# Down projection of a mixture of experts with the tokens stationary and w_down streaming, on one Trainium2 core

## The reference

```python
logits = (xf @ w_router + b_router).astype(jnp.float32)      # xf = rmsnorm(x), (1024, 1024)
top_logits, top_idx = lax.top_k(logits, TOP_K)               # 4 of 32
top_w = jax.nn.softmax(top_logits, axis=-1)
...
def expert_block(args):
    xb, e = args
    gu = xb @ w_gate_up[e] + b_gate_up[e]
    gate = jnp.minimum(gu[:, 0::2], SWIGLU_LIMIT)
    up = jnp.clip(gu[:, 1::2], -SWIGLU_LIMIT, SWIGLU_LIMIT)
    hidden = (up + 1.0) * gate * jax.nn.sigmoid(SWIGLU_ALPHA * gate)
    return hidden @ w_down[e] + b_down[e]
...
y = jax.ops.segment_sum(y_slots * slot_w[:, None], slot_tok, num_segments=t)   # x + y is the result
```

## Time and profile before

| | |
|---|---|
| Median of three runs | 2355.8 us (2354.04 to 2357.43) |
| The profiled execution | 2354.11 us, span 2352.3 us, granted clock 0.986 |
| PE busy | 2256.7 us, 96% of the span |
| DVE, ACT, POOL busy | 940.0, 459.4, 222.8 us |
| DMA | 504.04 MB, mean 214 GB/s |
| Loop over blocks | from 672.7 us to the end |

### The profile page before, as it was taken

One profiled execution on the slowest core, in us unless ns is written; L12 is line 12 of the kernel. 1 busy time (PEld: TensorE's weight loads), 2 busy tenths in 40 slices (PEclk: granted clock), 3 DMA queues, 4 the chain that ended last, 5 costly groups with the idle time before them and its releaser, 6 DMA issues.

```text
span 2352.3 us, 43438 instructions
## 1 busy us (share of the span) xinstructions
PE 2256.7 (96%) x17777; PEld 2150.1 (91%) x17778; DVE 940.0 (40%) x2192; ACT 459.4 (20%) x848; POOL 222.8 (9%) x172
## 2 busy tenths in 40 slices
PE   6999998999969999999999999999999999999997
PEld 5878887778869999999999999999999999999997
DVE  6434434885363333233333333333333333333332
ACT  4243233664111111111111111111111111111110
POOL 1101100100001100001011000100010010001001
PEclk9999999999979999999999999999999999999999
DMA  4222221205377887788888878887888887888882
GB/s 164 99 72 72 90 81 61 75 3 196 129 230 250 276 282 239 238 274 263 290 278 278 281 239 274 266 279 228 289 273 290 277 255 236 285 290 271 290 274 36
DMA packets 250614, 504.04 MB, mean 214 GB/s; under 512 B 7994, under 2 KB 36718, under 8 KB 250238
## 3 DMA queue, kind: packets, MB, share of 16 engines
q1 hardware_dynamic: 234268, 451.96, 55.1%
q0 software_dynamic: 14912, 45.71, 9.7%
q10 hardware_dynamic: 1344, 5.01, 0.7%
HBM read 469.46 MB, written 31.10 MB: 213 GB/s over the span
## 4 chain that ended last, share of the span: by engine, by line
PE 91%; DVE 4%; issue 3%; DMA 2%; ACT 1%; POOL 0%; DVEq 0%; ACTq 0%; SPq 0%; POOLq 0%
PE bank L1044 43%; PE bank L1055 19%; PE bank L802 12%; PE bank L1032 2%; DVE hx L1407 2%; PE bank L1003 2%; PE bank L913 2%; PE bank L900 2%; PE bank L947 1%; PE bank L948 1%; PE bank L949 1%; PE bank L995 1%; DMA mix<-xn_scratch,hx 1%; PE bank L884 1%; PE bank L810 1%
## 5 line engine op out<-in xcount | busy, mean ns | idle before, releaser
L1044 PE MATMUL bank<-hx,ring 128*128 128x140 f32 (+1 forms) x8192 | 1034.3, 288 | 21.9 <-issue 12.5
L1044 PEld LDWEIGHTS bank<-hx,ring 128*128 128x128 f32 x8192 | 1018.5, 197 | 28.6 <-issue 27.6
L1055 PE MATMUL bank<-hx,ring 128*128 128x140 f32 (+1 forms) x4096 | 514.8, 287 | 0.0
L1055 PEld LDWEIGHTS bank<-hx,ring 128*128 128x128 f32 x4096 | 507.0, 190 | 0.0
L758 ACT ACTIVATE hx<-hx 128x168 f32<-128x168 f32 x256 | 87.9, 343 | 1439.1 <-DVE hx L1478 1439.1
L1478 DVE TENSOR_SCALAR hx<-bank,hx 128x168 f32<-128x168 f32 x256 | 100.4, 392 | 630.6 <-PE bank L1044 630.0
L1503 DVE TENSOR_SCALAR hx<-bank,hx 128x168 f32<-128x168 f32 x256 | 100.4, 392 | 354.2 <-PE bank L1055 354.2
L571 POOL DMA_INDIRECT out_x<-mix,hx x66 | 99.8, 1511 | 815.9 <-ACT mix L751 775.7
L550 POOL DMA_INDIRECT mix<-xn_scratch,hx x66 | 65.0, 984 | 719.0 <-DVE hx L1402 708.9
L802 PE MATMUL bank<-hx_r,mix_r 128*128 128x512 f32 x480 | 115.7, 400 | 7.6 <-DVE hx_r L1138 7.6
L802 PEld LDWEIGHTS bank<-hx_r,mix_r 128*128 128x128 f32 x480 | 91.8, 193 | 28.2 <-issue 9.1
(11 more groups left out here) (201 smaller groups left out, 1715.0 us busy)
## 6 DMA issues: line engine op xcount, KB each, us to landing
ring<-in_w_gate_up SPq DMA_DIRECT2D x128, 2048.0 KB, 11.1
ring<-in_w_down SPq DMA_DIRECT2D x64, 2048.0 KB, 8.9
mix<-in_w_in SPq DMA_DIRECT2D x14, 1024.0 KB, 5.0
work<-in_w_in SPq DMA_DIRECT2D x14, 1024.0 KB, 5.0
ring<-in_x SPq DMA_DIRECT2D x8, 512.0 KB, 8.3
hx<-in_w_out SPq DMA_DIRECT2D x1, 4096.0 KB, 14.3
work<-in_x ACTq DMA_DIRECT2D x8, 512.0 KB, 4.9
out_x<-work SPq DMA_DIRECT2D x8, 512.0 KB, 4.4
```

What stands on the lines that cost most here:

```text
L1044: mm = e.matmul(bank[f % 2][:, part * CAP:part * CAP + w], gu_ring[:, k, f * 256 + part:(f + 1) * 256:2], xT[:, k, 0:w], start=k == 0, sto ...
L1055: return e.matmul(bank[2 + j % 2][:, 0:w], dn_ring[:, k, j * P:(j + 1) * P], hid[:, k, 0:w], start=k == 0, stop=k == KD - 1)
```

## The change

Down now has the hidden tokens stationary (128 of them) and w_down moving, 512 columns at a time, in two halves t of the output and eight steps k. Both operands are split into a high fp32r part and a low rest, and three fp32r products are summed (`down_main`). The high part of w_down is copied by ScalarE (`upper`), the low one made by VectorE (`lower`), both in the gate and up part of the same block; `hid` is split likewise (`hid_hi`, `hidden_low`). The result lies with tokens on the partitions, so `turn_rows` and `yT` go, and `weigh_rows` scales it straight out of PSUM. The bias b_down enters by one more product (`down_bias`, three bf16 parts picked by `sel`). Tokens past 128 are handled in groups of 32 (RO = 2 groups): `down_over` multiplies 32 stationary tokens with four quarters of w_down's columns, each quarter in its own 32 columns of the array and 32 partitions of bank 7, in float32, behind a branch on the number of tokens. So these tokens are gathered and scattered as quarter rows of 256 elements. `hot` grows to 3 x 128 slots; there are three indirect DMAs for two, and the gather stands ahead of the scatter. The list is made after f=3 and the one-hot behind f=1. `w_down` is loaded when the block before has done all of down. The widths 140 and 168 stay for gate and up, in two copies of the body.

The diff, cut to its core:

```diff
-        hid = region(hx, 0, KD, CAP)
+        hid = region(hx, 0, KD, SLOTS)
+        hid_lo = region(hx_r, 0, KD, SLOTS)[:, :, 0:P]
+        hid_hi = region(hx_r, 1536, KD, P)
+        hot = region(work[:, 8192:9728].bitcast(BF16), 0, NT, NH * P)
+        dn_hi, dn_lo = region(work_r, 0, 2, KD, CH), region(mix_r, 0, 2, KD, CH)
...
                 for c in range(2):
-                    e.wait_ge(m_dn, n * 8 + (4 * c - 4))
+                    e.wait_ge(m_dn, n * 2 + 2)
                     e.dma_start(dn_ring[:, :, c * 512:(c + 1) * 512], dn_r[x_e, c]).then_inc(dn_in[c], 16)
...
             def block_dmas(n):
-                add_rows(n)
                 e.wait_ge(l_ok, n + 2)
-                e.wait_ge(g_tr, n * 3 + 3)
+                e.wait_ge(sc_done, n * 48 + 48)
                 e.sem_inc(pool_go, 1)
                 gather()
+                add_rows(n)
...
+            def upper(n, q):
+                nh, k = q // 4, q % 4 * 2
+                if k == 0:
+                    e.wait_ge(dn_in[nh], n * 16 + 16)
+                e.activation(dn_hi[:, nh, k:k + 2], dn_ring[:, k:k + 2, nh * CH:(nh + 1) * CH], ACT.Copy).then_inc(c_hi, 1)
...
             def weigh_rows(n):
-                e.wait_ge(sc_done, n * 32 + 16)
-                for h in range(2):
-                    for q in range(2):
-                        m = 2 * h + q
-                        e.wait_ge(m_ytr, n * 4 + (m + 1))
-                        e.activation(yo[:, h, q * 512:(q + 1) * 512], bank[4 + m][0:HC, :], ACT.Copy,
-                                     scale=w_sc[:, h:h + 1]).then_inc(m_yo, 1)
+                e.wait_ge(l_keep, n + 1)
+                e.wait_ge(g_tr, n * 4 + 8)
+                for t in range(2):
+                    e.wait_ge(m_dn, n * 2 + (t + 3))
+                    e.activation(y_m[:, t * CH:(t + 1) * CH], bank[2 + t][:, :], ACT.Copy, scale=w_sc[:, 0:1]).then_inc(m_yo, 1)
+                for r in range(RO):
+                    e.activation(y_o[:, r], bank[7][:, r * 2 * P:(r + 1) * 2 * P], ACT.Copy,
+                                 scale=w_sc[:, 1 + r:2 + r]).then_inc(m_yo, 1)
...
                     e.activation(sg[:, f % 2], g1[:, f % 2], ACT.Sigmoid, scale=GALPHA).then_inc(m_sig, 1)
-                    if f == 0:
-                        weigh_rows(n)
+                    if f == 3:
+                        upper(n, 0)
+                    if 3 <= f < 7:
+                        upper(n, f - 2)
+                    e.wait_ge(m_hid, n * 8 + (f + 3))
+                    e.activation(hid_hi[:, f], hid[:, f, 0:P], ACT.Copy).then_inc(h_hi, 1)
+                for q in range(5, 8):
+                    upper(n, q)
+                weigh_rows(n)
...
+            def down_bias(t):
+                e.matmul(bank[2 + t][:, :], sel, bias_d[:, t * CH:(t + 1) * CH], start=True, stop=False,
+                         skip_group_check=True)
+            def over_bias():
+                for r in range(RO):
+                    for j in range(GR):
+                        e.matmul(bank[7][quarter_rows(j), r * 2 * P:(r + 1) * 2 * P], sel[:, 0:OV],
+                                 bias_d[:, j * 2 * P:(j + 1) * 2 * P], start=r == 0, stop=False, skip_group_check=True)
+            def down_main(n, t, k):
+                if t == 0:
+                    e.wait_ge(h_lo, n * 8 + (k + 1))
+                if k % 2 == 0:
+                    e.wait_ge(c_lo, n * 8 + (4 * t + k // 2 + 1))
+                for h, w in ((hid_hi, dn_hi), (hid_lo, dn_hi), (hid_hi, dn_lo)):
+                    mm = e.matmul(bank[2 + t][:, :], h[:, k], w[:, t, k], start=False, stop=k == KD - 1 and w is dn_lo,
+                                  skip_group_check=True)
+                if k == KD - 1:
+                    mm.then_inc(m_dn, 1)
+            def down_over(r):
+                for k in range(KD):
+                    for j in range(GR):
+                        e.matmul(bank[7][quarter_rows(j), r * 2 * P:(r + 1) * 2 * P],
+                                 hid[:, k, P + r * OV:P + (r + 1) * OV], dn_ring[:, k, j * 2 * P:(j + 1) * 2 * P],
+                                 start=False, stop=k == KD - 1, skip_group_check=True)
...
+                e.wait_ge(s_sel, n + 1)
+                down_bias(0)
...
+                down_bias(1)
+                for k in range(4):
+                    down_main(n, 1, k)
+                e.wait_ge(g_in, n * 48 + 96)
+                turn_tokens()
+                for k in range(4, KD - 1):
+                    down_main(n, 1, k)
+                e.wait_ge(l_ok, n + 2)
+                over_bias()
+                with e.If(tokens > P):
+                    down_over(0)
+                if w > P + OV:
+                    with e.If(tokens > P + OV):
+                        down_over(1)
+                down_main(n, 1, KD - 1)
...
+            def lower(n, q):
+                nh, k = q // 4, q % 4 * 2
+                e.wait_ge(c_hi, n * 8 + (q + 1))
+                e.tensor_tensor(dn_lo[:, nh, k:k + 2], dn_ring[:, k:k + 2, nh * CH:(nh + 1) * CH],
+                                dn_hi[:, nh, k:k + 2].bitcast(F32), ALU.subtract).then_inc(c_lo, 1)
...
+                    if f == 3:
+                        lower(n, 0)
+                    if 3 <= f < 7:
+                        lower(n, f - 2)
```

More of the change, by code:

```diff
@@ L50 @@
 NE = 32
+OV = 32
+GR = P // OV
+RO = 2
 CAP = 168
-HC = CAP // 2
+SLOTS = P + RO * OV
+NH = 1 + RO
 TOPK = 4
@@ new lines, in layer @@
+        tw_s = region(hx[:, 7444:7444 + NT * 5 // 2].bitcast(BF16), 0, NT, 5)
+        pos_s = region(hx, 7464, NT)
+        pos_t = region(small, 840, NT)
+        it_base = region(hx, 7472, NI)
+        it_low = region(hx, 7472 + NI, NI)
+        it_f = region(hx, 7472 + 2 * NI, 2, NI)
+        it_i = region(hx, 7472 + 4 * NI, 2, NI).bitcast(I32)
+        btab = region(small, 224, NE, 16)
+        be = region(small, 736, 16)
+        l_raw = region(small, 752, NH)
+        idx = small[:, 756:756 + NH].bitcast(U32)
@@ L556, in _ @@
             e.wait_ge(e_st[1], 128)
-            e.dma_start(b_rows[:, 2048:3072], b_down[0]).then_inc(sc_done, 16)
+            for g in range(3):
+                e.dma_start(b_raw[g * NE:(g + 1) * NE], b_down[0]).then_inc(sc_done, 16)
             e.wait_ge(l_ok, 1)
@@ L992, in token_list @@
             def token_list():
-                for h in range(2):
+                for h in range(NH):
                     for i in range(NT):
-                        mm = e.matmul(bank[7][0:HC, 5 * h:5 * h + 5], hot[:, i, h * HC:(h + 1) * HC], tw_s[:, i, :],
+                        mm = e.matmul(bank[7][:, 5 * h:5 * h + 5], hot[:, i, h * P:(h + 1) * P], tw_s[:, i, :],
                                       start=i == 0, stop=i == NT - 1)
@@ L1104, in _ @@
                     block_pe(n)
-            turn_rows(more + NE)
         @block.vector
@@ L1438, in _ @@
             e.wait_ge(bias_ok, 3)
-            for m in range(3):
-                e.wait_ge(g_tr, m + 1)
+            for g in range(1, 3):
+                e.wait_ge(b_cast, g)
+                rows = slice(0, 3 * NE) if g == 1 else slice(2 * NE, 3 * NE)
+                e.tensor_tensor(b_raw[rows], b_raw[rows], bias_d[rows], ALU.subtract).then_inc(b_sub, 1)
+            for m in range(4):
+                e.wait_ge(g_tr, m + 1 if m < 2 else 4)
                 tokens_out(m)
-            for s_ in (m_up, m_gs, m_hid):
+            for s_ in (m_up, m_gs, m_hid, m_dn):
                 e.sem_inc(s_, 2)
+            e.sem_inc(m_yo, 4)
             grid = [P, NX, NE]
@@ L1499, in block_dve @@
                         list_out(n + 1)
-                e.wait_ge(m_ytr, n * 4 + 4)
-                for j in range(KD):
-                    e.wait_ge(m_dn, n * 8 + (j + 1))
-                    e.tensor_scalar(yT[:, j, :], bank[2 + j % 2][:, 0:CAP], be[:, 16 + j:17 + j], None, ALU.add)\
-                        .then_inc(m_y, 1)
-                    if j == 6:
-                        for m in range(3):
-                            e.wait_ge(g_tr, n * 3 + (m + 4))
-                            tokens_out(m)
+                hidden_low(n, KD - 1)
+                for q in range(5, 8):
+                    lower(n, q)
+                for m in range(4):
+                    e.wait_ge(g_tr, n * 4 + (m + 5 if m < 2 else 8))
+                    tokens_out(m)
             with e.Fori(0, NE) as n:
```

272 lines of the change are left out of this document (136 added, 136 removed).

## The result

The kernel after takes 2245.5 us (median of four runs, 2241.65 to 2247.83) against 2354.9 of the kernel before in the same session (2353.76 to 2357.43). The ratio is 0.9533, with an interval of 0.9521 to 0.9545: 4.7% faster. The forecast was 2260 with a range of 2240 to 2325, so the time lies in the range, 15 us under the forecast. The profiled execution took 2247.8, span 2246.0, against 2354.1 and 2352.3 before: 106.3 us of span less.

The account below looks back on a forecast made before the run. PE's own list was taken as the bound. Gains of 14 x 4.8, 13 x 0.9 and 18 for the wide blocks sum to 97 us; 2354.1 less 97 is 2257, taken as 2260, range 2240 to 2325.

Parts of the forecast that it names:

- second group of the 165 block: A second `down_over` call in the one block with more than 160 tokens, taken at 3.9 us.
- idle issue behind wide blocks: PE's idle issue at a wide block's end: 1.0 us left of the 1.96 now, in each of five blocks.
- What bounds it: PE's own list is the chain of waits, TensorE busy 96% of the span; a block is the sum of PE's pieces.
- the step on which it hung: In `down_over`, four column quarters overlap as two halves do: 3.9 us a call, 3.5 if all four overlap, 14.0 serially.
- The fp32r products: In `down_main`, 48 products of 512 columns a block at 0.2267 us each, 10.88 in all.
- the list: PE's part of making the list, each block: 24 small products for 16 which took 0.61, taken at 0.92 us.
- `over_bias`: Eight bias products of 256 columns in four column groups, every block: 0.9 us serially, 0.25 four at a time, taken 0.5.
- the branches: Branches in PE's loop body, each block: 0.1 us taken, 0 to 1.96 possible.
- rival 3: Waits in every block from late code, weights or DVE; 1.96 us in 27 more blocks, +53, 2313 us; chance 0.15.
- The cover: Added DVE (18 to 30 us a block), ACT (6 to 17) and transfer work costed at nothing; up to 64 us if gone.
- rival 4: DMA becomes the bound: by packets 51.0 us a narrow block, 103 more than the sum, 2363 us; chance 0.03.
- The ends: Kernel start 4 us later, finish 4 less (14.3 for 18.7 after the last product), so they cancel.

## Why the prediction was right, point by point

The loop's part of the sum, forecast against the trace of after (first product of block 0 to the last product):

| term | forecast | measured |
|---|---|---|
| 14 blocks up to 128 tokens | 45.3 each | 44.45 |
| 13 blocks of 129 to 140 | 49.2 each | 47.92 |
| 5 wide blocks, products alone | 55.2 each | 53.9 |
| second group of the 165 block | 3.9 | 3.46 |
| idle issue behind wide blocks | 5.0 | 16.5 |
| lower clock behind them | 0 | 11.7 |
| block 0, and the blocks at either end, beyond their kind | 0 | 9.2 |
| sum | 1558.7 | 1555.6 |

The 16.5 are what the block lengths leave; the four pieces of issue add up to 15.9, and each is 0.16 short, since a next product otherwise starts that much before the end of the last.

So 1555.6 for 1558.7 is errors that nearly cancel, and that is luck: 35 us too much on the blocks' own work, 23 too little behind the wide ones and 9 at the ends. The 9.2 are hardly a loss of the change: block 0 lasted 56.48 before and lasts 55.07 after. The kernel before had the like, some 8 us, which stood in its span. The forecast itself was a difference to that span, 97 us less; the pair of profiled executions shows 106.3 less, 105.3 in the loop and 1.0 at the ends. So the gain was 9.3 larger than forecast. The rest of the 15 us is 3 of rounding up to 2260 and 2.3 by which the profiled execution lies above the median.

**What bounds it** held: PE is the whole chain before and after. Every record removed came back at its price (12 transposes 1.31; 16 fp32r products 3.58). PE's idle time is in no block put down to ACT, DVE or DMA, except 1.5 in block 0, where DVE has only just made its tables.

**`down_over`, the step on which it hung**, held and to the lower bound: 3.46, where 3.9 was taken and 3.5 given as the end for all four. The step from halves to quarters was right. The page TensorE: Matmul & The Clock Gate of the Trainium skill gives, under "Measured speedup vs the span model", 2.38 times for three column tiles, from which the estimate was 4.4; here four quarters of float32 are at full rate. What the prediction didn't say is that the order of the loops is part of it: k outside and the quarters inside.

**The fp32r products** held: 24 in 5.46 are 0.2275 each for 0.2267, and all 48 in a block up to 128 tokens are 11.19 with the passing to quarters and back in them (5.46 + 2.75 + 2.09 + 0.89), for 10.88 + 0.2. Too dear were the list (0.59 for 0.92: 24 records cost no more than 16 did, so the price was not by the record), `over_bias` (0.33 for 0.5), the branches (0.1, none seen) and gate and up, 15.25 + 15.37 = 30.62 for 30.90. In the earlier trace rows gate and up came in three pieces, at 0.1275, 0.1193 and 0.1209 a record; now there are two, at 0.1191 and 0.1201, so a piece has a lead-in of its own that the turning back had added. All this is 0.85 a block, and with `down_over` 1.3.

**Behind the wide blocks lies the term that was most wrong in size.** One us of the 1.96 was left, behind each of five. Measured are 3.12 behind the 165 block, 4.13 to 4.31 behind three others and none behind the fifth, and in the block that follows a gap 2.8 to 3.0 more, since PE comes back at the lower clock: block lengths of 50.90 for 47.92 and 47.38 for 44.45. The mechanism stood in the prediction, under rival 3, but as a danger to the narrow blocks; there it didn't come. Two statements beside it were wrong. PE's loop does not keep its length (1784 for 1728), though this isn't what lengthened the gap, since the same 36 packets are fetched. And the gap is no fixed price of a jump: 5.3 to 6.2 us run from the first packet to the next product, and the new block leaves PE 1.3 us of work beside them where the old one left 4.0 to 4.2. The experiments with a shorter loop take the whole of it away. Which blocks of code are thrown out, and where between 1516 and 1680 the fetching begins, was not tried; nor is it shown why the wide block behind the 165 one has no gap.

**The cover** was rightly sized and wrongly placed. DVE 28.6 us a block for 30, ACT 15.8 for 17, `lower` 1223 ns and `upper` 1042 for 1.22 and 1.05. The prediction saw 3 us in hand, at f=2; at least 7.7 us more, spread over the block, fit under gate and up, and the thin place is the way from its end into `down_main`. The DMA share of 0.93 in a block of 44.44 us is 41.3, for 43.2 forecast from the earlier trace rows by bytes and 51.0 by packets (rival 4). The indirect queue alone has 13.3% of blocks that last 48 us on the mean, 6.4 us, where by packets it would be 15.6. So quarter rows don't cost as much as whole ones.

**The ends** did not cancel as told. At the start 0.9 later, not 4: the last gather's landing took 3.7 us, not 6.9. At the end the chain of waits has

```profile
2228.25 0.91 PE bank L1099 x3
...
2231.44 0.86 POOL out_x L603
...
2235.26 1.56 POOL out_x L606
```

From the last product (2229.16) to the last issue 6.1 us pass, against 6.2 forecast. But everything ends 10.7 later, not the 8.1 taken over from the earlier trace rows: 16.8 for 14.3, and 18.7 before. A scatter's median from issue to landing is 9.5 in the loop, 7.3 before. Start and end together gained 1.0.

## What to carry to other kernels

Where fewer than 128 stationary columns are left over, split the moving side into column groups and issue neighbours in different groups: the same products cost 3.46 or 11.31 us by the order of two loops. Count the instructions of a loop with branches over all copies of its body before adding a copy or a width, and keep what doesn't depend on the branch outside it; here that was worth 22 us, and one copy too many cost 267. Where a jump must fetch code, dear work just ahead of it hides the fetch and cheap work doesn't. A sum over TensorE's records was good to 3% a block here; the surprises stood where PE has nothing to do, so look at those first.

## What the runs showed of the hardware that was not expected

- Code fetches for TensorE's loop come in steps: none at 1400 and 1516 products and loads, 36 packets in each of the six kernels from 1680 to 1784, 149 at 2076, with single gaps around 17 us.
- From the first code packet at a jump to the next product 5.3 to 6.2 us passed, and PE's work in hand (1.1 to 4.2 us) ran beside them.
- After a gap of 4.3 us the granted clock was 0.50 for the next 3.8 us and 0.65 on the mean of 3.0 more, so that the gap cost 2.8 to 3.0 us beyond itself.
- A product of 128 float32 columns with its own weights takes 0.1177 us, hardly less than one of 140 (0.1191), while 168 take 0.1425: below 140 something other than the columns sets the time. Transposes of 128 columns go at 0.109.
- When column groups are issued one after another, each change saves about the time of four records: 11.31 for 13.8 and 6.08 for 6.9.
- With a DMA share of 1.01 a block had no wait for a transfer.
